# Recurrent gates of an RG-LRU as 64x64 matrix products on four quarters of the TensorE array, with a copy of each chunk whose halves are exchanged

## The reference, cut to what matters

```python
LRU_BLOCKS, LRU_BLOCK = 8, 64
xc = _dwconv(r_x, conv_w, conv_b)                 # (B, T, 512)
def _rglru_dir(x, w_a, b_a, w_x, b_x, lam, h0):   # once for each of two directions
    xb = x.reshape(B, T, LRU_BLOCKS, LRU_BLOCK)
    r = jax.nn.sigmoid(jnp.einsum('btnd,nde->btne', xb, w_a).reshape(B, T, D_GROUP) + b_a)
    i = jax.nn.sigmoid(jnp.einsum('btnd,nde->btne', xb, w_x).reshape(B, T, D_GROUP) + b_x)
    log_a = -LRU_C * r * jax.nn.softplus(-lam)
    a = jnp.exp(log_a)
    u = jnp.sqrt(jnp.maximum(-jnp.expm1(2.0 * log_a), 0.0)) * (i * x)
    ...                                           # then h = scan(a, u)
```

## Time and profile before

| | us |
|---|---|
| median of 3 runs | 732.19 (731.52 to 733.46) |
| the profiled execution, whole | 731.01 |
| its span, first to last instruction | 729.3 |
| PE busy | 676.2 (93%), mean granted clock 0.975 |
| DVE busy | 579.7 (79%) |
| ACT busy | 441.6 (61%) |
| POOL busy | 56.9 (8%) |

### The profile page before, as it was taken

One profiled execution on the slowest core, in us unless ns is written; L12 is line 12 of the kernel. 1 busy time (PEld: TensorE's weight loads), 2 busy tenths in 40 slices (PEclk: granted clock), 3 DMA queues, 4 the chain that ended last, 5 costly groups with the idle time before them and its releaser, 6 DMA issues.

```text
span 729.3 us, 12727 instructions
## 1 busy us (share of the span) xinstructions
PE 676.2 (93%) x4906; PEld 560.1 (77%) x4906; DVE 579.7 (79%) x844; ACT 441.6 (61%) x612; POOL 56.9 (8%) x88
## 2 busy tenths in 40 slices
PE   4699999999899999999979999999999999999881
PEld 2487998898688989956868788888888888888640
DVE  2739998798994367678488998999999999999765
ACT  1537867363232455693134689888888888888731
POOL 2060000000011010122002300000000000000310
PEclk9799999999999999999989999999999999999996
DMA  9999496645767699949916999999999999999432
GB/s 322 357 253 330 174 360 228 221 145 196 274 244 243 208 391 377 342 162 294 285 32 274 337 398 399 399 400 399 401 399 400 399 400 399 400 399 400 167 128 86
DMA packets 91324, 219.17 MB, mean 301 GB/s; under 512 B 3339, under 2 KB 3635, under 8 KB 91271
## 3 DMA queue, kind: packets, MB, share of 16 engines
q1 hardware_dynamic: 84928, 199.24, 74.3%
q0 software_dynamic: 5840, 18.94, 8.0%
q10 hardware_dynamic: 503, 0.28, 0.1%
HBM read 179.08 MB, written 39.36 MB: 300 GB/s over the span
## 4 chain that ended last, share of the span: by engine, by line
PE 73%; DVE 18%; ACT 3%; DMA 3%; issue 2%; SPq 1%; DVEq 0%; ACTq 0%
PE ps L1214 70%; DMA ring<-in_w_in 3%; PE ps L1654 2%; DVE w_lo L1817 2%; DVE arena L1977 1%; DVE arena L1976 1%; PE ps L1673 1%; DVE arena L1922 1%; DVE w_lo L2296 1%; ACT w_hi L843 1%; SPq L562 1%; DVE arena L2184 1%; DVE arena L2165 1%; DVE arena L2390 1%; DVE arena L2160 1%
## 5 line engine op out<-in xcount | busy, mean ns | idle before, releaser
L2296 DVE TENSOR_TENSOR w_lo<-ring,w_hi 128x1024 fp32r<-128x1024 f32 x96 | 114.7, 1220 | 8.9 <-ACT w_hi L1098 7.9
L2296 DVE TENSOR_TENSOR w_lo<-arena,w_hi 128x1024 fp32r<-128x1024 f32 x96 | 114.6, 1220 | 8.6 <-ACT w_hi L1098 7.1
L1098 ACT ACTIVATE w_hi<-ring 128x1024 fp32r<-128x1024 f32 x96 | 100.6, 1062 | 19.7 <-PE ps L1214 19.3
L1098 ACT ACTIVATE w_hi<-arena 128x1024 fp32r<-128x1024 f32 x96 | 101.1, 1064 | 14.9 <-PE ps L1214 14.7
L1214 PE MATMUL ps<-h_hi,w_lo 128*128 128x384 f32 x288 | 101.4, 352 | 8.6 <-DVE w_lo L1817 6.9
L1214 PE MATMUL ps<-w_hi,slot_tokens_lo 128*128 128x512 f32 x256 | 102.7, 401 | 1.2 <-DVE w_lo L2296 1.1
L1214 PE MATMUL ps<-w_hi,slot_tokens_hi 128*128 128x512 f32 x256 | 100.2, 391 | 0.0
L1214 PE MATMUL ps<-w_lo,slot_tokens_hi 128*128 128x512 f32 x256 | 99.8, 390 | 0.0
L1214 PE MATMUL ps<-h_hi,w_hi 128*128 128x384 f32 x288 | 97.2, 338 | 0.0
L1214 PE MATMUL ps<-h_lo,w_hi 128*128 128x384 f32 x288 | 97.1, 337 | 0.0
L1817 DVE TENSOR_TENSOR w_lo<-ring,w_hi 128x1024 fp32r<-128x1024 f32 x44 | 53.6, 1225 | 23.9 <-ACT w_hi L843 22.9
(11 more groups left out here) (393 smaller groups left out, 1166.9 us busy)
## 6 DMA issues: line engine op xcount, KB each, us to landing
slot_rows<-arena SPq DMA_DIRECT2D x12, 2048.0 KB, 17.9
ring<-in_w_in SPq DMA_DIRECT2D x11, 2048.0 KB, 10.3
ring<-in_w_ada SPq DMA_DIRECT2D x10, 2048.0 KB, 9.2
ring<-in_w_gate SPq DMA_DIRECT2D x8, 2048.0 KB, 18.3
ring<-in_w_up SPq DMA_DIRECT2D x8, 2048.0 KB, 20.6
arena<-in_w_up SPq DMA_DIRECT2D x8, 2048.0 KB, 20.6
ring<-in_w_down SPq DMA_DIRECT2D x8, 2048.0 KB, 15.2
arena<-in_w_gate SPq DMA_DIRECT2D x8, 2048.0 KB, 18.2
```

The costliest lines, as they stand in the source:

```text
L1098: act.activation(w_hi[:, at_ % 4, :], raw[:, q * QUARTER:(q + 1) * QUARTER], ACT.Copy).then_inc(S["hi_ready"], 1)
L2296: tt(w_lo[:, at_ % 4, :], raw[:, q * QUARTER:(q + 1) * QUARTER], w_hi[:, at_ % 4, :].bitcast(F32), ALU.subtract).then_inc(S["lo_dve"], 1)
```

## The change

For each chunk, direction and gate the 128x128 block-diagonal product becomes two products of 64x64, one for each block b of the chunk. Gate g reads its weights and its data from partitions 64g to 64g+63, and block b is written to partitions 64b to 64b+63 of PSUM, so that the four products of a direction lie on the four quarters of the array. Where b and g differ, the block's data lie in the wrong half of the partitions. So POOL makes, with two DMAs for each chunk, a copy of `XC` with its halves exchanged (`XC_SWAP`, two buffers), after `rx_conv` and after the chunk before has been copied; from chunk 2 on also after PE has used the buffer. PE's `lru_mm` waits for that copy. The weights need no zeros any more, so the two memsets go; the eight weight DMAs keep their sizes and have other destinations.

```diff
-        w_bd = [arena[:, at_:at_ + 1024].rearrange("p (g c e) -> p g c e", g=2, c=C) for at_ in (15 * U, 12 * U)]
+        w_gates = [arena[:, at_:at_ + 512].rearrange("p (c b e) -> p c b e", c=C, b=2) for at_ in (15 * U, 12 * U)]
+        XC_SWAP = [unit(u, 512, T) for u in (15, 12)]
...
-            for d in range(2):
-                pool.memset(w_bd[d], 0.0).then_inc(S["lru_zeroed"], 1)
-            pool.wait_ge(S["lru_zeroed"], 2)
             for x in range(len(EARLY_ADA)):
                 pool.wait_ge(early_in[x], 16 * len(early_at[x]))
...
-                        pool.dma_start(w_bd[d][64 * b:64 * b + 64, g, :, 64 * b:64 * b + 64], src).then_inc(S["lru_w_in"], 16)
+                        pool.dma_start(w_gates[d][64 * g:64 * g + 64, :, b, :], src).then_inc(S["lru_w_in"], 16)
...
             pool.tensor_copy(hg_masks.rearrange("p d l t -> p (d l t)"), masks_wide).then_inc(S["masks_cast"], 1)
+
+            for c in range(C):
+                pool.wait_ge(S["rx_conv"], c + 1)
+                if c:
+                    pool.wait_ge(S["xc_swapped"], 32 * c)
+                if c >= 2:
+                    pool.wait_ge(S["gates_ready"], 2 * c - 2)
+                for b in range(2):
+                    pool.dma_start(XC_SWAP[c % 2][64 * b:64 * b + 64, :], chunk(XC, c)[64 - 64 * b:128 - 64 * b, :]).then_inc(S["xc_swapped"], 16)
...
                     pe.wait_ge(S["rx_conv"], c + 1)
+                    pe.wait_ge(S["xc_swapped"], 32 * (c + 1))
                     for d in range(2):
-                        for g in range(2):
-                            last = mm(ps[:, 3 + 3 * d + g, 0:T], w_bd[d][:, g, c, :], chunk(XC, c))
+                        for b in range(2):
+                            for g in range(2):
+                                src = (chunk(XC, c), XC_SWAP[c % 2])[b ^ g]
+                                rows = slice(64 * g, 64 * g + 64)
+                                last = mm(ps[64 * b:64 * b + 64, 3 + 3 * d + g, 0:T], w_gates[d][rows, c, b, :], src[rows, :])
                         last.then_inc(S["gates_ready"], 1)
```

More of the change, by code:

```diff
@@ L84 @@
     "out_small out_S out_C out_y z_ready lam_abs lam_exp z_taken consts_made y_hi pos_added cols_ready mod1_ready h_hi "
-    "rx_conv sp_ready lru_zeroed gates_ready gates_taken lru_act lru_den lru_sqrt lru_done tok_taken rows_zeroed gate_rows gcol_zeroed gcol_in bulk ones_ready "
+    "rx_conv sp_ready xc_swapped gates_ready gates_taken lru_act lru_den lru_sqrt lru_done tok_taken rows_zeroed gate_rows gcol_zeroed gcol_in bulk ones_ready "
     "dve wout_used sco_top sco_full hg_start hg_scores hg_taken hg_fwd hg_bwd hg_final kb_T kb_T_sb s_fin s_fin_sb o_ready o_sq o_sum o_rstd o_T yh_done "
```

## The result

The changed kernel takes 738.62 us (median of 6 runs, 736.99 to 740.52), the kernel before beside it 732.61 (6 runs, 731.52 to 734.8). The ratio is 1.0078, with an interval of 1.0059 to 1.0096: 5.7 us slower, where 2.3 was forecast. The time lies 0.6 us above the range, so the prediction is wrong, though its sign was right. The profiled execution of after took 736.99 us, 735.3 of it span: 6.0 more than the span of before.

A forecast was written before the change was run, and what follows sets the result against it. PE was taken to bound the kernel, busy 93% of the span. Stall +3.8, clock +2.2 and four shorter jobs -3.7 gave +2.3 us on 732.2, so 734.5; the eight-in-ten range was 729.5 to 738.0.

The forecast's parts named there:

- The working of the products: Eight smaller products per chunk in `lru_mm` take 1.41 us in place of 2.33; bounds 1.41, 2.33 and 4.7.
- stall: PE waits at chunk 0's `lru_mm` for the copy: +3.8 us; landings of 3.9 to 8.8 give 1.1 to 6.0.
- clock behind it: PE's granted clock falls after the wait at chunk 0, costing +2.2 us; bounds 0 and 3.1.
- four shorter jobs: The changed products of all four chunks together save 3.7 us of PE time.
- The list of what would make the prediction wrong: Copy landing before 62, clock staying at 1.00, or ACT or DVE absorbing part of the delay between 76 and 104.
- rivals 3 and 4: Changed products: only column groups overlap, 738.2, chance 0.12; or quarters run one after another, 747.5, chance 0.02.
- PE feeds ACT by way of `gq[2]`: ACT waited 3.11 us for PE there, so each microsecond PE gains or loses earlier should move the end.
- convolved by 77 us: Chunks 2 and 3 are convolved by then and wanted after 115, so waiting for their copies costs nothing.
- Rival 2: At chunk 0 the copy inside SBUF is quick, no stall comes and the whole gain stands: 728.5; chance 0.12.
- Chunk 1 had no stall, as the sum said: Chunk 1's extra wait of 0.7 us falls away, since the slower clock brings PE there after its copy.
- rival 1: At chunk 0 the stall comes but the clock holds: 733.0; chance 0.23.
- ACT's chain: ACT's `L924`, at 75.77 before, was expected at about 79.9 (3.8 + 2.2 less 1.9).

The follow-up runs named there:

- half shift: Kernel before with 32 small float32 products (128 instructions) added behind PE's first transpose: 737.3 us, ratio 1.0059.
- third experiment: Changed kernel without the copies and without PE's wait for them (gates not the reference's): 735.04 us, ratio 1.0036.
- half change: Changed kernel with quarters for chunks 2 and 3 alone and 56 small products added: ratio 0.9994; with one projection unit moved as well, 0.9989.
- the shift alone: Kernel before with 130 waits, already met, added ahead of PE's first product: 738.03 us, ratio 1.0095.
- shift-back run: Changed kernel with 191 more already met waits in PE's list, to shift later instructions by 256: 737.52 us, ratio 1.0070.

## Why the prediction was wrong, point by point

**The step that failed** is the one that isn't there. The working of the products ends with their length on PE, and the sum has three terms: stall, clock behind it, four shorter jobs. It gives the added instructions no place in the stream. Shifting them back is worth 1.0078 - 1.0017 = 0.0061 of the time, 4.5 us (2.5 to 6.4 by the two intervals); the same shift in the kernel before costs 732.21 x 0.0095 = 7.0 us, a half shift 4.3. The list of what would make the prediction wrong doesn't have it either. The trace of before had one line on it: "issue" as what ended 0.25 us of idle time at 137.07, which also stands as the start of a piece in the chain. I took 137.07 as a boundary of PE's runs and did not ask what "issue" was.

**The other terms** come out of the runs like this.

- *The products.* 1.41 was taken, 1.45 measured (116.46 to 117.91), so two rounds of four quarters do run side by side, and rivals 3 and 4 are out. Eight products of 384 columns at the 0.58 that one took alone before are 4.6 us: 3.2 times faster. The Trainium skill ("TensorE: Matmul & The Clock Gate", Measured speedup vs the span model) has 3.07 for four row tiles; this trace is near it with two rows by two columns. The gain is 4 x (2.33 - 1.45) = 3.5 us of PE time, as forecast.
- *What the gain is worth.* The sum took all of it, on the ground that all four jobs lie in PE's runs. Without copies (third experiment) 1.77 us of 3.5 are there at `diag`. I argued that PE feeds ACT by way of `gq[2]`, and so each microsecond moves the end. But `lru_act` 0 has a second condition: in the kernel ACT waits there for `rx_conv` of all four chunks. DVE's last `conv` and the first row of `lru_act` before, then ACT's without copies:

```profile
74.25 2.69 DVE L1901 SCALAR_TENSOR_TENSOR arena<-arena,small 128x126 f32<-128x126 f32 x6
77.32 1.28 ACT L949 ACT_TABLE_LOAD   x1
```

```profile
77.42 1.28 ACT L947 ACT_TABLE_LOAD   x1 [1.56 <-DVE arena L1902]
```

  Before, DVE was done at 76.94, 0.38 us ahead of `lru_act`, so no more than about 0.4 of the gain of chunks 0 and 1 could pass. Without copies ACT has its data from PE 1.44 us earlier (74.33 in place of 75.77), then stands 1.56 us for DVE, and PE's second run starts at 104.65, where it started at 104.55. The prediction has "convolved by 77 us" in it, but as a condition of the copies only. Chunks 2 and 3 keep their gain: the half change has 1.6 of 1.8. This term was mis-sized: about 2 us in place of 3.7 in the stretch, and 1.1 over the whole kernel.
- *The stall.* Forecast 3.8, measured 2.98. PE came to the job at 62.33 in place of 61.98, and the halves landed 5.2 us after their issue, not 6.6. POOL's timeline and the landing of the first two (KB each, median us from issue to landing):

```profile
59.28 1.07 POOL L711 DMA_DIRECT2D arena<-arena  x2 [2.39 <-DVE arena L1913]
arena<-arena POOLq DMA_DIRECT2D x2, 96.0 KB, 5.2
```

  A row between the two bounds of 3.9 and 8.8, nearer to the short one than I chose. Rival 2 is out at this place, because of the load and not of the kind of copy: 5.2 us are 1.2 less than the fastest load took under it, and 2.0 were enough with the engines idle. The Trainium skill ("DMA: Bandwidth & Descriptors", Anatomy of one DMA) made 2.2 us an estimate for it: the 2.0 agree with that, the 5.2 under load do not. Chunk 1 had no stall, as the sum said.
- *The clock behind the stall.* Forecast 2.2. In the profile of after it stayed at 1.00. PE's windows around the stall:

```profile
62.00:64.00 2.00, 0.33 (x6) 0.00 (x0) 1.83 (x5) 1.98 (x4) 0.00 (x0) 1.00 1.08 394
64.00:66.00 2.00, 0.69 (x9) 0.44 (x13) 1.85 (x5) 1.94 (x4) 0.28 (x1) 1.00 1.03 329
```

  It stayed there also with the stream shifted back by products, and with the copies from ACT's queue, and fell in two others (2.84 and 4.51 us for jobs of 1.52 and 2.85: 1.3 and 1.7 us). So it is real in some executions and not in others: rival 1 was the truth of this profile, the forecast that of others. The cost of the wait as a whole, measured at 2.3 us (0.6 to 4.0), is less than the 6.0 of stall and clock together. A part is DVE's again: 1.56 us of the stall fall into time that ACT would have waited for `conv`. In the stretch the shifted-back change takes 146.9 us and the same without the wait 145.6, so 1.3 for a stall of 2.95 at full clock. The runs of the shifted-back change spread over 7 us (730.22 to 737.53), those without the wait over 5 (728.52 to 733.37); that the clock makes the difference fits, but is not shown: the one profile of the shifted-back change is of an execution of 730.68 us, near the low end.
- *ACT's chain.* Expected at 79.9. ACT's timeline of after:

```profile
77.07 0.58 ACT L932 ACTIVATE arena<-ps,small 128x384 f32<-128x384 f32 x1 [2.41 <-PE ps L1222]
```

  77.07, which is 1.30 later than before. The forecast of +4.1 was 3.8 + 2.2 less 1.9. With the measured terms it is 0.35 (PE's later arrival) + 2.98 + 0 less two jobs of 0.9, so 1.5: the way of reckoning was right, with two terms off.

**The split that the runs give**, by the ratios against the kernel before: the smaller products alone -1.1 us (no copies, shifted back), the wait +2.3 (the change shifted back less that), the shift +4.5 (the change less the change shifted back). That the three add up to the 5.7 measured follows from how they are taken; what the runs settle is the share of each. Without copies on both sides the shift comes out at 3.7. The first two make +1.2 where the forecast had +2.3, from a gain too large and a loss too large that partly cancelled each other: that these two terms came near was luck. The change without its shift would have lain within the bound of no change.

**What stays open.** Why a piece is fetched only when it is: the transfer of after starts by 134.1, 0.4 us before PE's last small pass is over (134.49), and not earlier. Why the shift alone shows one stop of 2.33 us where after shows three, yet costs as much or more over the whole (1.0095 against 1.0078): 1.5 us of its profile are lost outside the stretch, what is left of rows that went both ways, and I did not follow them. And whether any form of the change is worth having: the two half changes lie at 0.9994 and 0.9989, with intervals that hold 1.

## What to carry to other kernels

Adding instructions to an engine moves all its later ones within the pieces in which its program is brought in; where dense groups of very short products come later, look whether the trace has "issue" stops there before and after, and test it by a harmless shift of the unchanged kernel. When a change makes PE's work shorter but adds a wait for a transfer ahead of the first use, apply it only to the uses that come late enough for the transfer. And where a gain has to pass to another engine, look up everything that this engine waits for there: the gain is worth no more than the time to the next of these conditions, here 0.4 us of 1.8.

## What the runs showed of the hardware

- PE stopped at places 127 passes apart (about 254 instructions), while a queue of kind "instruction" brought 34 transfers of 16 KB. At the first stop of after PE went on 2.3 us after the transfer had started. Behind passes of 256 columns 0.25 to 0.92 us of it showed at `diag`, in groups of 32-column passes 0.8 to 2.3.
- Waits whose conditions hold are not free on PE. Two of the added waits became one instruction, by the passes that the stops moved: 32 for 130 waits, where one instruction each would have made it 65. With 65 such instructions ahead of it PE's first product stood at 9.35, with 95 at 12.59: (12.59 - 9.35) / 30 = 108 ns each. The two rows, PE's timeline of the shift alone and of the change shifted back by waits:

```profile
9.35 0.26 PE L1328 MATMUL ps<-small,arena 16*128 16x16 f32 x1 [9.35 <-issue]
```

```profile
12.59 0.25 PE L1336 MATMUL ps<-small,arena 16*128 16x16 f32 x1 [12.59 <-issue]
```

- Eight float32 products of 64x64 weights and 384 columns on the four quarters took 1.45 us, two rows by two columns of the array at a time.
- Copies of 96 KB inside SBUF landed 4.1 to 6.2 us after their issue in after, where other transfers kept the DMA engines busy, and 2.0 us after it in the shift-back run, issued with the engines idle. Under load, a copy from ACT's queue let PE go on no sooner than one from POOL's.
- A stall of 2.5 to 3 us took the granted clock down to about 0.5 for some microseconds in two of the profiles and left it at 1.00 in three others.
